# A hybrid encoder block on one core: order of copies and weight splits in the delta-rule mixer

## What is computed

```python
h = rmsnorm(x);  z = h @ w_in                      # 13 kinds of columns, 11,296 in all
q, k, v = silu(causal_conv4(z_q, z_k, z_v))        # mixer A: 8 heads, keys and values 128 wide
# per head and block of tokens, A strictly lower triangular:
T = inverse(I + A);  u = T @ (v * beta);  w = T @ (k * beta * exp(gc))
v_new = u - w @ S;  o = (q * exp(gc)) @ S + (q k^T * decay) @ v_new
S = S * exp(g_last) + k_dec^T @ v_new
# mixer B: gated linear attention, 4 heads;  then
x = x + (sigmoid(mix_a) * (oa @ w_oa) + sigmoid(mix_b) * (ob @ w_ob)) @ w_out
x = rmsnorm(x + mixture_of_experts(rmsnorm(x)))    # 32 experts, 2 for each token
```

## Time and profile before

| what | us |
|---|---|
| median of 3 executions | 1831.14 |
| lowest and highest | 1829.31, 1833.02 |
| the profiled execution's own time | 1828.15 |
| span of its trace, first to last instruction | 1826.1 |
| PE busy in the span | 1750.8 |
| DVE, ACT busy | 677.2, 443.8 |
| mean granted clock of PE | 0.976 of full |

### The profile page before, as it was taken

One profiled execution on the slowest core, in us unless ns is written; L12 is line 12 of the kernel. 1 busy time (PEld: TensorE's weight loads), 2 busy tenths in 40 slices (PEclk: granted clock), 3 DMA queues, 4 the chain that ended last, 5 costly groups with the idle time before them and its releaser, 6 DMA issues.

```text
span 1826.1 us, 21030 instructions
## 1 busy us (share of the span) xinstructions
PE 1750.8 (96%) x8774; PEld 1123.6 (62%) x8774; DVE 677.2 (37%) x740; ACT 443.8 (24%) x483; POOL 181.0 (10%) x223
## 2 busy tenths in 40 slices
PE   8999999999989999999999999999999999999996
PEld 7888878887878788888644444444444444444442
DVE  5357767545744454553221222202222122211222
ACT  6354455234532343333200000000000000000002
POOL 4000032420052100000000000000000000000001
PEclk9999999999989999999999999999999999999999
DMA  7454435324432455566999999999999999999997
GB/s 241 159 164 160 161 115 185 116 93 137 151 104 93 111 178 190 175 229 252 369 414 409 426 428 428 428 429 428 429 429 428 430 428 428 430 427 429 428 427 286
DMA packets 95003, 537.41 MB, mean 294 GB/s; under 512 B 5772, under 2 KB 5836, under 8 KB 69980
## 3 DMA queue, kind: packets, MB, share of 16 engines
q1 hardware_dynamic: 94352, 535.85, 74.0%
q0 software_dynamic: 592, 0.69, 0.3%
HBM read 534.42 MB, written 2.10 MB: 294 GB/s over the span
## 4 chain that ended last, share of the span: by engine, by line
PE 86%; DMA 5%; DVE 3%; ACT 2%; issue 1%; POOL 1%; DVEq 0%; SPq 0%; ACTq 0%; POOLq 0%
PE psum L1975 22%; PE psum L1519 12%; PE psum L1521 12%; PE psum L1520 12%; PE psum L2002 11%; PE psum L1900 6%; DMA arena<-in_w 5%; PE psum L2020 2%; PE psum L2021 2%; PE psum L1741 1%; DVE y_lo L1458 1%; ACT w_hi L703 1%; PE psum L1733 1%; PE psum L1939 1%; DVE w_lo L1037 1%
## 5 line engine op out<-in xcount | busy, mean ns | idle before, releaser
L1975 PE MATMUL psum<-arena 128*64 128x512 f32 x2048 | 443.9, 593 | 1.8 <-DMA arena<-in_w 1.3
L1037 DVE TENSOR_TENSOR w_lo<-arena,w_hi 128x2048 fp32r<-128x2048 f32 x119 | 273.3, 2299 | 226.9 <-ACT w_hi L703 218.1
L1519 PE MATMUL psum<-w_hi,hT_hi 128*128 128x512 f32 x824 | 332.9, 404 | 2.6 <-DVE arena L1293 1.4
L1520 PE MATMUL psum<-w_lo,hT_hi 128*128 128x512 f32 x824 | 328.2, 398 | 0.0
L1521 PE MATMUL psum<-w_hi,hT_lo 128*128 128x512 f32 x824 | 328.2, 398 | 0.0
L1975 PEld LDWEIGHTS psum<-arena 128*64 128x64 f32 x2048 | 145.3, 137 | 289.5 <-issue 285.4
L703 ACT ACTIVATE w_hi<-arena 128x2048 fp32r<-128x2048 f32 x119 | 227.5, 1915 | 336.5 <-PE psum L1521 323.6
L2002 PE MATMUL psum<-arena 128*64 128x512 f32 x960 | 209.7, 594 | 0.7 <-DMA arena<-in_w 0.7
L1519 PEld LDWEIGHTS psum<-w_hi,hT_hi 128*128 128x128 f32 x824 | 156.6, 190 | 39.5 <-issue 2.0
L1521 PEld LDWEIGHTS psum<-w_hi,hT_lo 128*128 128x128 f32 x824 | 156.1, 189 | 38.1
L1520 PEld LDWEIGHTS psum<-w_lo,hT_hi 128*128 128x128 f32 x824 | 156.6, 190 | 35.9
(11 more groups left out here) (365 smaller groups left out, 1419.6 us busy)
## 6 DMA issues: line engine op xcount, KB each, us to landing
arena<-in_w SPq DMA_DIRECT2D x186, 2048.0 KB, 21.3
arena<-in_w_in SPq DMA_DIRECT2D x87, 1024.0 KB, 5.0
arena<-in_w_out SPq DMA_DIRECT2D x16, 1024.0 KB, 5.0
arena<-in_w SPq DMA_DIRECT2D x12, 1024.0 KB, 17.9
arena<-in_w_oa SPq DMA_DIRECT2D x8, 1024.0 KB, 5.0
arena<-in_w_ob SPq DMA_DIRECT2D x8, 1024.0 KB, 5.0
arena<-in_x SPq DMA_DIRECT2D x4, 1024.0 KB, 7.7
out_y<-arena SPq DMA_DIRECT2D x4, 512.0 KB, 4.0
```

Of the source, the lines that this page charges most:

```text
L1037: tt(w_lo[x % RING_A], ringA[:, x % RING_A, :], w_hi[x % NSPLIT].bitcast(F32), ALU.subtract)\
L1519: mm(m_banks[m], lhs[0][:, k0 + k, ms], wh[:, cs], start=(start and k == 0), stop=False)
L1520: mm(m_banks[m], lhs[0][:, k0 + k, ms], wl[:, cs], start=False, stop=False)
L1975: i = mm(bank(w)[e * CAP:(e + 1) * CAP, :], xeT[u][:, k, e * CAP:(e + 1) * CAP], src[e][:, (k % 8) * CB:(k % 8 + 1) * CB], start=(k == 0), ...
```

## The change

It has six parts. (1) At the start ACT splits chunk 3 between the two sums of squares. (2) In `obT` DVE no longer splits between the two results. (3) In the inverse ACT copies both halves of `Y` first and splits and evacuates afterwards (except at the first level, where it stays ahead), and DVE splits after the `dU` subtraction. (4) The chunk that stood behind `wT` in each group stands behind `Y1`. (5) `u0` comes before `wT`; the copies of the state products have no split between them on either engine; PE opens `v1` with the four products that do not need the state and then runs the four that do. DVE's split that stood ahead of `oi` now follows the `o` copies. (6) The merge starts without the wait for `oaT`.

```diff
--- before.py
+++ after.py
@@ -77,7 +77,7 @@
              + [f"lv{b}" for b in LEVELS] + ["kd", "bS", "bo0", "bo1", "obT0", "obT1"])
 GDN_STEPS = (["zqT", "zkT", "zvT", "gcb", "ssq", "ktok", "vtok", "khT", "A", "PT", "Y1"]
              + [f"{w}{b}" for b in LEVELS[1:] for w in ("Tt", "Y", "dU") if b > 2 or w != "Tt"]
-             + ["wT", "u0", "S", "v1", "oi", "o", "oaT"])
+             + ["u0", "wT", "S", "v1", "oi", "o", "oaT"])
 STEPS = GLA_STEPS + [f"{s}.{g}" for g in range(NG) for s in GDN_STEPS]
 
 FIRST_BLOCKS = 2
@@ -88,10 +88,10 @@
 ] + [
     {f"{k}.0": v for k, v in
      {"gcb": 9, "ssq": 2, "vtok": 1, "khT": 1, "PT": 1, "dU2": 1, "dU4": 1, "dU8": 1, "dU16": 1, "dU32": 1,
-      "dU64": 1, "wT": 1, "o": 3}.items()},
+      "dU64": 1, "Y1": 1, "o": 3}.items()},
     {f"{k}.1": v for k, v in
      {"gcb": 8, "ssq": 1, "vtok": 1, "khT": 1, "PT": 0, "dU2": 1, "dU4": 1, "dU8": 1, "dU16": 1, "dU32": 1,
-      "dU64": 1, "wT": 1, "o": 2}.items()},
+      "dU64": 1, "Y1": 1, "o": 2}.items()},
 ]
 
 
@@ -754,6 +754,8 @@
             for m in range(NM):
                 nc.scalar.activation(Z1[:, m * D:(m + 1) * D], xs0[:, m, :], ACT.Square,
                                      accum_out=ss1[:, m:m + 1]).then_inc(sem("ss1"), 1)
+                if m == 0:
+                    sp_.follow(1)
             act.wait_ge(sem("small_in"), SMALL)
             nc.scalar.activation(small_w[0], wsm[:, 0:KT * NSM], ACT.Copy).then_inc(sem("small_split"), 1)
             sp_.follow(FIRST_BLOCKS * BCH)
@@ -855,23 +857,24 @@
                 result("khT" + s)
                 nc.scalar.activation(T_["zT1"][:, 0:1024], pair("khT" + s), ACT.Copy).then_inc(sem("khT"), 1)
                 for i, b in enumerate(LEVELS[1:]):
-                    sp_.before(f"Y{b}" + s)
+                    if i == 0:
+                        sp_.before(f"Y{b}" + s)
                     act.wait_ge(sem("Y_half"), g * 6 + i + 1)
                     nc.scalar.activation(T_["Y"][:, 0:512], pair(f"Y{b}" + s)[:, 0:512], ACT.Copy)\
                         .then_inc(sem("Y"), 1)
                     wait(act, full(f"Y{b}" + s))
                     nc.scalar.activation(T_["Y"][:, 512:1024], pair(f"Y{b}" + s)[:, 512:1024], ACT.Copy)\
                         .then_inc(sem("Y"), 1)
+                    sp_.before(f"Y{b}" + s)
                     sp_.rest()
-                result("wT" + s)
+                result("u0" + s)
+                nc.scalar.activation(T_["T"][:, 0:512], pair("u0" + s)[:, 0:512], ACT.Copy).then_inc(sem("u0"), 1)
+                wait(act, full("wT" + s))
                 nc.scalar.activation(T_["nwT"], pair("wT" + s)[:, 0:512], ACT.Copy, scale=-1.0)\
                     .then_inc(sem("wT"), 1)
-                result("u0" + s)
-                vn = units(T_["T"])
-                nc.scalar.activation(T_["T"][:, 0:512], pair("u0" + s)[:, 0:512], ACT.Copy).then_inc(sem("u0"), 1)
-                result("S" + s)
+                wait(act, full("S" + s))
                 nc.scalar.activation(T_["aS"], pair("S" + s)[:, 0:512], ACT.Copy).then_inc(sem("a_S"), 1)
-                result("v1" + s)
+                wait(act, full("v1" + s))
                 nc.scalar.activation(T_["T"][:, 512:1024], pair("v1" + s)[:, 0:512], ACT.Copy).then_inc(sem("v1"), 1)
 
                 nc.scalar.activation(T_["L1"], Zb[:, 3 * 1024:4 * 1024], ACT.Tanh, scale=0.5).then_inc(sem("tz"), 1)
@@ -1183,7 +1186,10 @@
             i.then_inc(sem("b_out"), 1)
             dve.wait_ge(sem("small_in"), SMALL)
             for i in range(2):
-                result(f"obT{i}")
+                if i:
+                    wait(dve, full(f"obT{i}"))
+                else:
+                    result(f"obT{i}")
                 for hf in range(2):
                     src = pair(f"obT{i}").rearrange("p (h f t) -> p h f t", h=2, f=2)[:, :, hf, :]
                     dst = obT[:, 4 * i:4 * i + 4, :].rearrange("p (h f) t -> p h f t", f=2)[:, :, hf, :]
@@ -1263,22 +1269,23 @@
                 for i, b in enumerate(LEVELS[1:]):
 
                     if i:
-                        result(f"Tt{b}" + s)
+                        wait(dve, full(f"Tt{b}" + s))
                         dve.wait_ge(sem("T"), 6 * g + i)
                         nc.vector.tensor_copy(T_["T"], pair(f"Tt{b}" + s)).then_inc(sem("T"), 1)
-                    result(f"dU{b}" + s)
+                    wait(dve, full(f"dU{b}" + s))
                     dve.wait_ge(sem("U"), 7 * g + i + 1)
                     tt(T_["U"], T_["U"], pair(f"dU{b}" + s), ALU.subtract).then_inc(sem("U"), 1)
-                    sp_.rest()
-                result("oi" + s)
+                    sp_.before(f"dU{b}" + s)
+                wait(dve, full("oi" + s))
                 tt(units(T_["inter"], GH), units(pair("oi" + s)[:, 0:512], GH),
                    mh(eg)[:, 1, hs_g].unsqueeze(2).to_broadcast([P, GH, P]), ALU.mult).then_inc(sem("inter"), 1)
-                result("o" + s)
+                wait(dve, full("o" + s))
                 nc.vector.tensor_copy(u4(T_["Y"])[:, :, 0, :], u4(pair("o" + s))[:, :, 0, :])
                 dve.wait_ge(sem("inter"), g + 1)
                 tt(u4(T_["Y"])[:, :, 1, :], u4(pair("o" + s))[:, :, 1, :], units(T_["inter"], GH), ALU.add)\
                     .then_inc(sem("a_o"), 1)
 
+                sp_.before("o" + s)
                 dve.wait_ge(sem("tz"), g + 1)
                 link(stt(T_["L1"], T_["L1"], 1.0, Zb[:, 3 * 1024:4 * 1024], ALU.add, ALU.mult))
                 dve.wait_ge(sem("a_sq"), g + 1)
@@ -1759,18 +1766,21 @@
                     fill(step + s)
 
                 v = T_["zT2"]
+                per_head("u0", lambda o, hh, u0, u1: mm(o, T_["U"][:, u0], v[:, u0], start=True, stop=True))
                 per_head("wT", lambda o, hh, u0, u1: mm(o, kb[:, u1], T_["U"][:, u1], start=True, stop=True))
-                per_head("u0", lambda o, hh, u0, u1: mm(o, T_["U"][:, u0], v[:, u0], start=True, stop=True))
                 wait(pe, ("u0", g + 1))
                 per_head("S", lambda o, hh, u0, u1: mm(o, T_["kdec"][:, hh], T_["T"][:, hh], start=True, stop=True))
+                open_pair("v1" + s)
+                o = pair("v1" + s)
+                heads = [(slice(h * P, (h + 1) * P), slice((2 * h + 1) * P, (2 * h + 2) * P)) for h in range(GH)]
+                for hh, u1 in heads:
+                    mm(o[:, hh], T_["U"][:, u1], v[:, u1], start=(hh.start == 0), stop=False)
                 wait(pe, ("a_S", g + 1))
                 wait(pe, ("wT", g + 1))
-
-                def v1(o, hh, u0, u1):
-                    mm(o, T_["U"][:, u1], v[:, u1], start=True, stop=False)
-                    return mm(o, T_["nwT"][:, hh], T_["aS"][:, hh], start=False, stop=True)
-
-                per_head("v1", v1)
+                for hh, u1 in heads:
+                    i = mm(o[:, hh], T_["nwT"][:, hh], T_["aS"][:, hh], start=False, stop=(hh.stop == GH * P))
+                done("v1" + s, i)
+                fill("v1" + s)
                 per_head("oi", lambda o, hh, u0, u1: mm(o, c[0][:, u1], T_["aS"][:, hh], start=True, stop=True))
                 wait(pe, ("v1", g + 1))
                 wait(pe, ("PT", g + 1))
@@ -1782,7 +1792,6 @@
 
 
             x = CH_MIX
-            wait(pe, ("oaT", NG))
             pe.wait_ge(sem("z"), len(BLOCKS))
             oh = [t.rearrange("p (k t) -> p k t", k=A_HEADS) for t in o_hi]
             ol = [t.rearrange("p (k t) -> p k t", k=A_HEADS) for t in o_lo]
```

## The result

The changed kernel takes **1802.4 us** (median of 4 runs, 1801.6 to 1804.1), against 1830.7 us (1829.3 to 1833.0) for the kernel before. The ratio is 0.9852 with a 95% interval of 0.9836 to 0.9868, so the gain is 28.3 us, or 24 to 30 by the interval. The forecast was 1810 with a gain of 21.2.

What follows compares the result with a forecast made beforehand. PE was taken as the bound, busy 1750.8 of 1826.1 us, so gains come from its stops and the clock lost behind them; the terms sum to 21.2 us, 1831.14 - 21.2 = 1810 us, range 1804 to 1818.5.

Steps and rivals of the forecast that it cites:

- Start: At the fourth chunk, splitting chunk 3 between the squares removes PE's stop of 1.2 plus 0.16: gain 1.4 us.
- obT: At `zkT` and `gcb`, earlier copies replace the old stop by a new one of 1.7: gain 2.3 us.
- Chunk behind `Y1`: In the inverse, the moved chunk covers the stop behind `Y1`: gain 1.5 us in group 0, 5.4 in group 1.
- `Y` copies: In the inverse, copying `Y` first removes four stops of PE: gain 3.7 us.
- Tails: State products from `u0` to `o`, reordered to take 7.2 us: gain 2.3 us in group 0, 3.8 in group 1.
- Merge: At the merge, PE no longer waits for `oaT` but for the last block's evacuation: gain 0.8 us.
- (b): Rival at the experts: the weight stream sets the end and hides the gain, 1831 or 1829 us; chance 0.04.
- (c): Rival in the inverse: splits come too late, PE waits 4.3 us at each of 12 levels, 1862 us; chance 0.02.
- (d): Rival at `Y` and state-product copies: half of 3.7 and of each tail's 2.3 stays, 1814 us; chance 0.10.
- (a): Rival: clock still falls at `gcb`, behind `Y1`, in the tail, 1815 us; upwards, two falls missed, 1807; chance 0.16.

Runs made afterwards that it cites:

- part 3 alone: Kernel before with only the `Y` copies put ahead of splits and evacuations, and DVE's split behind the `dU` subtraction: 1826.61 us.
- part 4 alone: Kernel before with only the chunk behind `wT` moved behind `Y1`, in both groups: 1816.83 us.
- the five rounds: Changed kernel timed again, unchanged, in five rounds against the kernel before and beside two further variants: 1801.6 us, ratio 0.9856.

## Why the prediction was right in its parts and wrong in its size

- **Start, 1.4.** Mis-sized. The stop of 1.2 was the shortest of five recordings, short because the clock had fallen before it and PE came late. It measured 1.2 to 3.1, with a loss of clock behind it in three of them, and part 1 gained 2.8 to 6.0, on average 4.3. The mechanism was right: the split at 22.2 made the stop go.
- **obT, 2.3.** 2.2 measured between the first two traces, with the stop at `zkT` 0.22 for 0.3, a new one of 1.54 for 1.7, and a clock that stayed up, as assumed. But four of the six recordings with the old stop lose 3.4 us of clock there, not 1.7; the piece takes 192.8 on average without part 2, so it gained 2.9.
- **Chunk behind `Y1`, 1.5 and 5.4.** Measured by undoing it: 1.5 and 5.5. The clock fell behind `Y1` again with its stop, so its 2.1 us were rightly booked to that stop.
- **`Y` copies, 3.7.** 4.5 in the run of part 3 alone. The sum counted the levels with a stop and nothing at the others.
- **Tails, 2.3 and 3.8.** From `u0` to the next chunk it is 7.4 us for the 7.2 forecast, without stops. The parts depend on each other: part 4 alone lengthens the tail, because ACT's split meets the `u0` copy, and with the chunk back in the tail the wait ahead of the merge grows.
- **Merge, 0.8.** 0.8 measured. `oaT` waits 0.48 for DVE, 0.6 to 0.8 forecast, and the evacuation hides it.
- **Rivals.** (b) fell: the first expert load came 26.8 earlier and the end 26.5. (c) fell: no wait for low parts in the inverse. (d) fell: the copies gained more than reckoned. (a) fell as a loss; its upward half, priced at two losses of 1.7, came true and was too small.

**The step that failed** is how the sum books the clock, and with it the term *Start*. It took the stops and the losses of one recording as the kernel's own: 1.2 + 0.16 for the start, 4.1 us of clock in all (0.5 at `gcb`, 2.1 behind `Y1`, 1.5 in the tail), and for chance only "with two of them missed at another phase it would be 1807". Other stretches of the same trace show more (granted clock 0.69 at 314 to 325, behind `ssq` of group 0, and 0.72 at 504 to 516, at that of group 1), and the sum takes up none of it.

What the runs showed in its place: the mean granted clock is 0.974 to 0.979 in eleven executions of the kernel before and 0.979 to 0.984 in five of the changed one. The share not granted, times each span, is 43.7 us lost on average against 33.5, so 10.2 us of clock were won, not 4.1. The rest of the mean gain of 26.3 us, 16.1, answers to the 17.1 that the sum has for stops. This is an estimate, since clock lost while PE stands is counted and costs no time, but it puts the surplus down to clock, not to stops. By place, averaged over the recordings, the surplus is 2.9 at the start (4.3 less 1.4), 0.6 at obT (2.9 less 2.3), 0.9 in `Y1` to `o`, and 0.5 and 1.4 behind the two `ssq`: 6.3, where the medians have 7.1 and the five rounds 5.7. The last two pieces, 1.9 us, are ones that the change doesn't touch. Whether a kernel that comes to them earlier loses less there, or the few recordings happened to, stays open. So the mechanism of the stops was right; that the time fell outside the range came in part from which recording the terms were read from.

## What to carry to other kernels

Look at the granted clock over the whole length of a trace before pricing any stop, and list every fall with the work ahead of it: falls that the change doesn't touch decide how far the result strays from the sum, and a second recording of the same kernel shows which repeat. Ask too what ended a stop: if it was the landing of a transfer, a loss of clock ahead of the stop is hidden in it, and the stop looks shorter than it is worth. An engine that counts as busy may still lose its clock: it fell at 20 of 22 series of one-column products 3.6 us long, and cutting them in two with dense work between won 4.9 us (1.0 of it a stop), about as much as the whole of part 3. When a cover is moved, run the move alone once: whatever it had covered (here a split of ACT just ahead of a copy) shows at once.

## What the runs showed of the hardware

- Products of 128x128 weights with one moving column take 3.6 us for 32, about 0.11 us each, at a granted clock of 1.00, and in 9 of 11 recordings the clock falls 2.9 to 4.5 us after the first of them in group 0, with no stop of PE in the 50 us since `gcb`. In halves of 1.84 us with 5.7 us of dense products between, it fell in neither of two there.
- The loss at one place of one program varies from recording to recording by 3.1 us (28.7, 30.2 or 31.8 us for the same work), while stops repeat to 0.1 us, except one that a landing transfer ends (1.2 to 3.1). Two kernels that differ by less than some 3 us can't be ranked by single profiles.
- The stop of 1.54 us at `gcb` cost no clock in any of the five recordings that have it; those of 2.63 and 3.35 us did in every one that had them (six and five).
